# Row sums and gate applied per unit in the attention stage, meta keys padded to 128 rows, one loaded tensor in the stage behind it

## What is computed

```python
def attend(qn, qr, q_chunk):
    s = (einsum('bqhd,bkhd->bhqk', qn, k_nope) + einsum('bqhr,bkr->bhqk', qr, k_rope)) * scale
    s = jnp.where((key_chunk[None, :] <= q_chunk[:, None])[None, None], s, NEG_INF)
    p = jax.nn.softmax(s, axis=-1)
    return jnp.einsum('bhqk,bkhd->bqhd', p, v)
...
h = layer_norm(DN_ALPHA * h + (o * silu(z)) @ w_o, ln_g[0], ln_b[0])
b_gate, c_gate, u, z = jnp.split(h @ w_in, 4, axis=-1)
conv = sum_k pad(c_gate * u)[:, k:k + L] * conv_w[k]          # k = 0, 1, 2
h = layer_norm(DN_ALPHA * h + (b_gate * conv * silu(z)) @ w_out, ln_g[1], ln_b[1])
```

## Time and profile before

| | us |
|---|---|
| median of 3 runs | 3089.55 (3088.41 to 3097.22) |
| the profiled execution | 3079.74 |
| its span in the trace | 3078.0 |
| stage p, from the span's start | 0 to 637 |
| stage b | 637 to 1742 |
| stage c | 1742 to 2141 |
| stage d | 2141 to 2881 |
| stage e | 2881 to 3078 |

### The profile page before, as it was taken

How to read it: one execution, slowest core, us unless ns; L and a number is a source line. 1 busy time by engine, 2 the same in 40 slices (tenths; PEclk the granted TensorE clock), 3 DMA queues, 4 the chain that set the end, 5 groups by cost and what they waited for, 6 DMA issues and landing times. The chain is left out here.

```text
span 3078.0 us, 46496 instructions
## 1 busy us (share of the span) xinstructions
PE 2777.9 (90%) x17428; PEld 2494.4 (81%) x17428; DVE 1594.1 (52%) x3249; ACT 1182.6 (38%) x3001; POOL 709.2 (23%) x263
## 2 busy tenths in 40 slices
PE   5999999969999999999999675664999999999898
PEld 5898999968888888888888554553899888999687
DVE  5556540048888888888888444434311112111355
ACT  3342112247777777777777401001211111001211
POOL 0000000023333334332222034334111212121154
PEclk8999999989999999999999888787999999999999
DMA  3554342221211122211111154554311110110443
GB/s 132 186 166 151 118 133 89 74 80 43 50 43 44 43 51 53 47 38 37 37 37 38 29 141 129 146 140 146 103 41 34 41 34 26 35 34 27 144 143 123
DMA packets 249698, 246.43 MB, mean 80 GB/s; under 512 B 85552, under 2 KB 217008, under 8 KB 243056
## 3 DMA queue, kind: packets, MB, share of 16 engines
q1 hardware_dynamic: 249520, 244.07, 27.8%
HBM read 159.21 MB, written 84.81 MB: 79 GB/s over the span
## 5 line engine op out<-in xcount | busy, mean ns | idle before, releaser
L967 DVE TENSOR_TENSOR b_pt_lo<-b_transposed,b_pt_hi 128x384 fp32r<-128x384 f32 (+4 forms) x784 | 429.6, 564 | 79.3 <-ACT b_pt_hi L863 72.7
L41 PE MATMUL d_ring<-d_h_hi,d_w_hi 128*128 128x344 f32 (+1 forms) x1280 | 447.8, 350 | 22.4 <-POOL d_w_lo L1276 17.3
L853 ACT ACTIVATE b_p<-b_ring,b_nmax 128x384 f32<-128x384 f32 (+7 forms) x784 | 435.6, 563 | 64.1 <-DVE b_nmax L959 62.9
L42 PE MATMUL d_ring<-d_h_lo,d_w_hi 128*128 128x344 f32 (+1 forms) x1280 | 449.0, 351 | 0.0
L43 PE MATMUL d_ring<-d_h_hi,d_w_lo 128*128 128x344 f32 (+1 forms) x1280 | 447.0, 349 | 0.0
L863 ACT ACTIVATE b_pt_hi<-b_transposed 128x384 fp32r<-128x384 f32 (+4 forms) x784 | 378.9, 503 | 168.8 <-PE b_transposed L896 132.3
L954 DVE TENSOR_REDUCE b_cmax<-b_ring 128x1 f32<-128x384 f32 (+4 forms) x736 | 396.0, 543 | 68.1 <-PE b_ring L43 58.2
L896 PE MATMUL b_transposed<-identity,b_p 128*128 128x128 f32 (+2 forms) x2448 | 384.5, 273 | 17.1 <-DVE b_pt_lo L967 9.3
L913 PE MATMUL b_o_ps<-b_pt_hi,b_v 128*128 128x256 f32 (+3 forms) x1280 | 353.2, 303 | 6.4 <-DVE b_o_t L974 3.6
L41 PE MATMUL b_ring<-b_k_hi,b_q_hi 128*128 128x384 f32 (+7 forms) x784 | 306.5, 391 | 30.9 <-DVE b_q_lo L931 21.2
L896 PEld LDWEIGHTS b_transposed<-identity,b_p 128*128 128x128 f32 (+2 forms) x2448 | 275.3, 135 | 62.1 <-issue 24.4
(11 more groups left out here) (159 smaller groups left out, 5112.6 us busy)
## 6 DMA issues: line engine op xcount, KB each, us to landing
p_x_raw<-x_a SPq DMA_DIRECT2D x24, 1032.0 KB, 5.3
queries<-p_stage SPq DMA_DIRECT2D x128, 129.0 KB, 2.1
d_w_st<-w_conv SPq DMA_DIRECT2D x32, 512.0 KB, 3.6
b_raw<-queries SPq DMA_DIRECT2D x15, 1032.0 KB, 5.1
keys<-p_stage SPq DMA_DIRECT2D x64, 129.0 KB, 4.2
gates<-p_stage SPq DMA_DIRECT2D x64, 129.0 KB, 2.0
b_raw<-keys SPq DMA_DIRECT2D x16, 516.0 KB, 4.9
values<-p_stage SPq DMA_DIRECT2D x32, 256.0 KB, 2.4
```

What stands on the lines that cost most here:

```text
L41: nc.tensor.matmul(out, w_hi, x_hi, start=start, stop=False)
L42: nc.tensor.matmul(out, w_hi, x_lo, start=False, stop=False)
L853: nc.scalar.activation(p[0:rows, n % PSLOTS, 0:w], banks[0:rows, n % RING, 0:w], ACT.Exp, bias=nmax[0:rows, tile % 8:tile % 8 + 1], accum_ ...
L967: nc.vector.tensor_tensor(pt_lo[part], tb[:, n % 2, 0:nb, 0:rows], pt_hi[part].bitcast(F32), ALU.subtract).then_inc(pt_split, 1)
```

## The change

1. Stage b: row sums are inverted for each unit (`inverse_sums(n)` right before the unit's last L): a sum of 128x2x(1 to 5), a reciprocal of 128x2, and for unit 0 a copy of the meta queries' sum. SyncE writes them to DRAM (`sums_out`: 256 pieces of 4 bytes, 16 more for unit 0), waits for the landing, and reads them back broadcast over 64 partitions (`sums_in`). It also loads the unit's gate (`gate_in`). GpSimd multiplies the unit's output by both (`gate(n)`), and SyncE stores the product (`output(n)`), one unit later in its order. GpSimd's splits now stand between the gates of the units: keys of the next head behind gate 3, queries behind gate 4, values behind gate 5, `w_o` behind gate 6.
2. One order for every head; the distance between letters is the same as before at the turn of a head (9 transposes and 6 products late).
3. The meta block of `b_v` is padded with zeros to 128 rows, and products use 128 rows for it too; transposed tiles lie packed.
4. Stage c loads the gated output alone, in three buffers, and the residual rows in three; GpSimd and VectorE no longer multiply there; `h_t` is stored from ScalarE's queue as soon as it is copied out.
5. Stage d: gates C and U are made in 5 pieces of 410 columns instead of 6 of 344 (the first 14 columns are left out), 18 groups, a ring of 6 banks.

```diff
+LAG = {"T": 9, "P": 6, "H": 6, "C": 1, "L": 10, "A": 2}
...
-                if more:
-                    next_keys(h)
-                output(h, 0)
-                if more:
-                    next_queries(h)
-                output(h, 1)
-                if h:
-                    sums(h - 1)
...
+            def sums_out(n):
+                sp.wait_ge(r_done, n + 1)
+                sp.dma_start(r_d[n:n + 1, 0:2 * P].rearrange("a (j p) -> p (a j)", p=P), r_sb[:, n % 4, 0:2], allow_slow_non_contiguous=True).then_inc(r_out, 16)
...
+            def sums_in(n):
+                w = unit_width(n)
+                sp.wait_ge(r_out, 16 * all_units(n))
+                if n >= 2:
+                    sp.wait_ge(weighted, n - 1)
+                sp.dma_start(r_all[half(n), 0:w], r_d[n:n + 1, 0:w].to_broadcast([64, w])).then_inc(r_all_in[n % 2], 16)
...
+            for n in range(HEADS * UNITS):
+                h, u = n // UNITS, n % UNITS
+                gate_in(n)
+                if h + 1 < HEADS and u == 2:
                     next_keys(h)
+                if h + 1 < HEADS and u == 4:
                     next_queries(h)
+                if h + 1 < HEADS and u == 5:
                     next_values(h)
+                if h < WO_PIECES and u == 6:
                     next_weights(h)
+                sums_out(n)
+                if n:
+                    output(n - 1)
+                sums_in(n)
...
+            def gate(n):
+                w = unit_width(n)
+                here = o_t[half(n), 0:w]
+                pool.wait_ge(o_done, n + 1)
+                pool.wait_ge(r_all_in[n % 2], 16 * (n // 2 + 1))
+                nc.gpsimd.tensor_tensor(here, here, r_all[half(n), 0:w], ALU.mult).then_inc(weighted, 1)
+                pool.wait_ge(z_loaded[n % 2], 16 * same_parity(n))
+                pool.wait_ge(weighted, n + 1)
+                nc.gpsimd.tensor_tensor(here, here, z_in[half(n), 0:w], ALU.mult).then_inc(gated, 1)
+                pool.wait_ge(gated, n + 1)
...
+            for n in range(HEADS * UNITS):
+                h, u = n // UNITS, n % UNITS
+                gate(n)
+                if h + 1 < HEADS and u == 3:
+                    split_keys(h + 1)
+                if h + 1 < HEADS and u == 4:
+                    split_queries(h + 1)
...
-                        nc.tensor.matmul(ob[:, part], v[0:keys, h % 2, vb, :], pt_hi[0:keys, n % 2, c, part], start=(x == 0 and c == 0), stop=False)
+                        nc.tensor.matmul(ob[:, part], v[:, h % 2, vb, :], turned(pt_hi, n, u, len(blocks))[:, c, part], start=(x == 0 and c == 0), stop=False)
...
+                then(nc.vector.reduce_sum(r_sb[:, n % 4, 0:2], csum[:, n % SUMS, 0:2, 0:len(UNIT_CHUNKS[u])], axis=AX))
+                nc.vector.reciprocal(r_sb[:, n % 4, tiles], r_sb[:, n % 4, tiles]).then_inc(r_done, 1)
...
-                sp.dma_start(o_in[:, i % 2, :, 0:n], o_d[:, :, t0:t0 + n].rearrange("k p t -> p k t")).then_inc(o_loaded[i % 2], 16)
-                sp.dma_start(s_in[:, i % 2, :, 0:n], z_d[:, :, t0:t0 + n].rearrange("k p t -> p k t")).then_inc(s_loaded[i % 2], 16)
-                for e in range(2):
-                    one = r_d.rearrange("(k e) t -> e k t", e=2)[e:e + 1, :, t0:t0 + n]
-                    sp.dma_start(r_in[64 * e:64 * e + 64, i % 2, :, 0:n], one.to_broadcast([64, KD, n])).then_inc(r_loaded[i % 2], 16)
...
+                if i >= 3:
+                    sp.wait_ge(gt_split, i - 2)
+                sp.dma_start(g_in[:, i % 3, :, 0:n], g_d[:, :, t0:t0 + n].rearrange("k p t -> p k t")).then_inc(g_loaded[i % 3], 16)
...
-CD = 344
-NCD = T // CD
-DRING = 5
...
+CD = 410
+NCD = (T - META + 2) // CD
+DRING = 6
```

More of the change, by code:

```diff
@@ L669, with steps @@
 PRODUCTS_PER_HEAD = len(PRODUCTS) // HEADS
[L672 to L679, removed]
-    return out
-TENSOR_STEPS, SCALAR_STEPS, VECTOR_STEPS = steps(TENSOR_ORDERS), steps(SCALAR_ORDERS), steps(VECTOR_ORDERS)
+def steps(order):
+    count = {}
+    lagging = [n < LAG.get(letter, 0) for i, letter in enumerate(order) for n in [order[:i].count(letter)]]
+    first = [letter for letter, late in zip(order, lagging) if not late]
+    last = [letter for letter, late in zip(order, lagging) if late]
+    out = []
+    for letter in first + list(order) * (HEADS - 1) + last:
+        n = count.get(letter, 0)
+        count[letter] = n + 1
+        out.append((letter, n))
+    return out
+SUMS = 5
+TENSOR_STEPS, SCALAR_STEPS, VECTOR_STEPS = steps(TENSOR_ORDER), steps(SCALAR_ORDER), steps(VECTOR_ORDER)
 WO_PIECES = KD
 def stage_b(nc, ident, wo_hi, wo_lo, dram):
-    k_d, kr_d, v_d, q_d, w_o, ident_d, o_d, r_d = dram
+    k_d, kr_d, v_d, q_d, z_d, w_o, ident_d, r_d, g_d = dram
     with ExitStack() as ctx:
@@ new lines, in _ @@
+            none = zero[:, 0:1].to_broadcast([P, 2 * VH])
+            for par in range(2):
+                nc.gpsimd.tensor_tensor(v[:, par, 0, :], none, none, ALU.add).then_inc(v_zeroed, 1)
+            def gate(n):
[8 more added lines that the diff above has]
+                pool.wait_ge(gated, n + 1)
@@ L1055, in _ @@
             load(0)
             load(1)
+            load_rows(0)
+            load_rows(1)
+            load(2)
             sp.dma_start(gb_ln[:, :, :], ln.to_broadcast([P, 2, D])).then_inc(ln_in, 16)
-            for i in range(2, NTC):
-                load(i)
-                store(i - 2)
-                if i >= 4:
-                    store_t(i - 4)
+            for i in range(NTC):
+                if i + 3 < NTC:
+                    load(i + 3)
+                if i + 2 < NTC:
+                    load_rows(i + 2)
+                if i >= 2:
+                    store(i - 2)
@@ L1081, in affine @@
-            def affine(i):
+            pool.wait_ge(ln_in, 16)
+            for i in range(NTC):
                 n = tokens(i)[1]
@@ L1124, in _ @@
                     gate_hi(i + 2)
-                if i >= LAG:
-                    turn(i - LAG)
+                if i >= LAG_C:
+                    turn(i - LAG_C)
+            for n in range(2):
+                act.wait_ge(ht_out[n], 16 * ((NTC - 1 - n) // 2 + 1))
         @block.tensor
```

307 lines of the change are left out of this document (143 added, 164 removed).

## The result

The changed kernel takes 3462.76 us, median of four runs (3460.09 to 3467.98), beside 3088.98 us for the kernel before on the same chip: ratio 1.1212, with a 95% interval of 1.1179 to 1.1244. It is 12% slower, where 2963 was forecast in a range up to 3030. The profiled execution has a span of 3460.9 us.

What follows compares the result with a forecast made beforehand. Stage c was taken as bound by its loop through the gated output, stage b by TensorE. 3079.7 - 157 - 11 - 10 - 50 + 102 = 2953.7, plus 9.8 up to the median: 2963 us, range 2860 to 3030.

Steps and rivals of the forecast that it cites:

- the price of the store of 256 pieces: Stage b, sums store to DRAM: 3.0 us, by count between 1.9 and 10.8 for 2064 pieces.
- The other links are covered: Stage b: apart from the queries' chain no wait is added; A's awaited store lands 1 to 3 us ahead or more.
- the late stores' rival: SyncE's wait in `sums_in`: 4-byte stores land in 10.8 us whatever their number, 15.6 us more a head, 3197 us; chance 0.09.
- The chain to the queries: Stage b, unit 3's sums to queries' split: 33.6 us for 28.4 available; TensorE waits 5.2 at 15 turns, with clock +102.
- The padding: Stage b, meta products on 128 rows instead of 16: 0.39 us less a unit, -50 us in 16 heads.
- The order of letters: Stage b: near the old order (44 VectorE steps at the turn of a head, 43 before), costed at nothing.
- my 2862 to 2877: Rival, stage b: no wait of TensorE for the queries, total time 2862 to 2877 us; chance 0.29.
- Stage c: Loop through the gated output goes, TensorE sets the pace: 220 us from first matmul instead of 378, -157 us.
- the rival in which 130 GB/s sets the pace: Stage c: DMA at 130 GB/s makes a tile 16.1 us instead of 12.0, +66, total time 3029 us; chance 0.07.
- the one in which the gated output is not what frees it: Stage c: something else keeps the loop at its length, total time 3120 us, slower by 1%; chance 0.03.
- Stage d: 1920 matmuls of 410 columns at 0.186 us replace 2304 of 344 at 0.16: -10 us (-3 to -14).
- Between b and c: Last sums leave earlier, so stage c's first matmul stands at 1752 instead of 1763: -11 us (-4 to -14).

Runs made afterwards that it cites:

- with rows: Changed kernel, each sums store replaced by the same 1 KB in rows of 512 bytes from a constant tile, every wait kept: 2925.06 us.
- experiment 2: Separate kernel timing stores alone and beside an output store: 128 pieces of 4 bytes took 7.9 us side by side, 1.40 us at 32 bytes distance.
- experiment 9: Padding of meta products added to the kernel before: 3055.66 against 3082.27 us; taken out of the kernel with rows and splits one unit earlier: 2870.02 against 2842.91.
- the world without waits: Changed kernel with sums stored as rows of 512 bytes of a constant tile and splits one unit earlier: 2842.91 us, ratio to before 0.9223.
- the other order of splits: Changed kernel with a partition's two sums stored side by side, keys loaded behind unit 1, split behind unit 2, queries split behind unit 3: 2904.9 us.

## Why the prediction was wrong

*The step that failed* is the price of the store of 256 pieces, "By count I take 3.0". It measured 9.5 us alone and 9.0 from `sums_out` to `sums_in` in the median unit. I drew a line through 1.9 us for a plain store and 10.8 for 2064 pieces. Time does not go by count here, and the plain store was no lower end for this one, since it has no pieces that share 32 bytes; my own upper end, 10.8, was near the truth. The rival with this price named the place, SyncE's wait in `sums_in`, and the point of decision (a landing of about 7 us), though not the cause, and had a chance of 0.09. Its argument against, "that one had eight times the pieces", was the same interpolation once more.

*The step "The other links are covered"* failed with it, and made the loss 524 us (stage b after, 1631.8, less 1107.6 with rows) where the late stores' rival had 234 more than the forecast. The rival charged two landings a head, on the chain to the queries. There are eight, one in each round of SyncE, and they alone bring a head of 66.7 us to over 72. The rival also left out the clock: of the 524 us, 389 are idle time of TensorE and 135 more busy time, at a granted clock of 0.84 instead of 0.97. And it took only SyncE's wait as the way in which a late store hurts. Without that wait the run is still 345 us above the one with rows, because stores and loads behind the sums are held as well, A's buffer among them. A sign of that stood in the earlier trace rows: at 1108.60 an A of the kernel before waited 2.10 us for a store of output, 17 us after the sums' store of that head was issued at 1091.29. I used it for the clock alone. Whether those sums held it was not tried; in the kernel before with the padding, where these landings can be read, the output stores next to the sums and to the loads of queries and values mostly landed after 5 to 12 us, and all others after 1.9 to 2.1.

*The two statements that I weighed for this store* are those of the Trainium skill, DMA: Bandwidth & Descriptors. The "~2.0 µs" fixed of section Anatomy of one DMA, given there for DMAs that GpSimd issues, compare with 1.1 to 1.9 us for the plain stores here from SyncE's queue, and with 8.3 us for this one from GpSimd's (median of six in experiment 2). The read-modify-write under Specifications pointed the right way and deserved the chance that I gave to the count; but its bound of 512 bytes is not what these runs show.

*The chain to the queries* was right in kind and nearly in size: 5.2 us a head forecast, 4.5 measured with rows (67.9 / 15), and with the clock and what follows 86 us for 102. The broadcast load in it, priced at 2.0, took 2.5 us alone and 2.7 in the median unit with rows, so that near agreement is in part luck. Had the store cost 3 us, the run would have been near 2925, against 2963.

*The padding* was the right mechanism in the wrong size: 27 us for 50. The 0.39 us came from one unit in which the 16-row product stood behind a score; the mean over 128 is 0.30. And of the 38 us of TensorE's time, 7 to 12 went to waits. In the kernel before, VectorE works 896 of 1083 us, and a shorter product runs into it, as the waits in experiment 9 show.

*The order of letters*, costed at nothing because one distance in it was the same, is worth up to about 31 us by subtraction. This and the padding err against each other, so that the world without waits came out at 2843, below my 2862 to 2877.

*Stage c* was right: -161 for -157, a tile at 11.78 for 12.0, and 216 us for 220 from its first matmul to the next stage's first instruction (2311.24 to 2526.87); DMA moved 167 GB/s there, so the rival in which 130 GB/s sets the pace falls, and so does the one in which the gated output is not what frees it. *Stage d*: -6 for -10, the step of 0.19 as forecast. *Between b and c*: -3 for -11. Two slow stores stand in that stretch: the last sums leave only at 2291.51, behind the wait for those before, and are read back at 2299.19. With rows it was -14 (10.4 for 24.5).

## What to carry to other kernels

Before a store of scattered elements goes into a loop, look at how many of its pieces fall into the same 32 bytes of DRAM, and measure that one store alone, in its own form; do not interpolate between others by count or bytes. A slow store in a round that repeats has to be charged once for each round, against the shortest time of the round, and then again for every transfer behind it, since taking the wait away doesn't free those. If values must leave one by one, keeping a partition's values together was worth 420 us here, with the other order of splits 558, and storing them twice on top 585. Whole rows were faster still, but they were stored from a constant tile: what transposing real sums into rows would cost was not measured.

## What the runs showed of the hardware

One store of 128 pieces of 4 bytes took 7.9 to 8.7 us with the pieces side by side and 1.40 us at a distance of 32 bytes or more; 32 pieces side by side took 3.7 and 64 took 6.7. 256 such pieces into SBUF took 1.9 us, and a load of 128 adjacent pieces 2.0, so it is the write to DRAM that is slow. While a store of 256 such pieces is in flight, a 1 KB store from another engine's queue took 6.4 to 8.8 us instead of 1.1 (23 of 24 times).
